# The HBM layout of a gate matrix G: by block of 32 tokens, expert row and expert against by expert row, expert and token

## The reference, cut to what matters

```python
va, ia = lax.top_k(sa, 16);  vb, ib = lax.top_k(sb, 16)       # 8 heads, product keys
top_s, pos = lax.top_k(va[..., :, None] + vb[..., None, :], 16)   # flattened over the pairs
experts = ia * 128 + ib                                        # the 8 * 16 = 128 picks of a token
gates = softmax(top_s)
act = gelu(einsum('tkd,td->tk', expert_u[experts], x))
out = einsum('tk,tkd->td', gates * act, expert_v[experts])
```

## Time and profile before

| what | value |
|---|---|
| median of three runs | 4338.44 us |
| the profiled execution, its own time | 4348.75 us |
| its span in the profile | 4346.7 us |
| mean granted TensorE clock | 0.906 of full speed |
| PE (TensorE) busy | 3666.6 us, 84% |
| DVE (VectorE) busy | 2812.8 us, 65% |
| POOL (GpSimd) busy | 1565.9 us, 36% |
| ACT (ScalarE) busy | 909.8 us, 21% |
| DMA queue q0 (issued by GpSimd) | 184336 packets, 666.53 MB, 41.1% of 16 engines' span |
| DMA queue q1 (issued by SP) | 194306 packets, 374.83 MB, 24.1% |

### The profile page before, as it was taken

One profiled execution on the slowest core, in us unless ns is written; L12 is line 12 of the kernel. 1 busy time (PEld: TensorE's weight loads), 2 busy tenths in 40 slices (PEclk: granted clock), 3 DMA queues, 4 the chain that ended last, 5 costly groups with the idle time before them and its releaser, 6 DMA issues.

```text
span 4346.7 us, 40408 instructions
## 1 busy us (share of the span) xinstructions
PE 3666.6 (84%) x13372; PEld 2071.1 (48%) x13372; DVE 2812.8 (65%) x5406; ACT 909.8 (21%) x1917; POOL 1565.9 (36%) x1400
## 2 busy tenths in 40 slices
PE   8999968888556667888569889999899899889995
PEld 6444435555343357788534334444344444434442
DVE  1222234567231127878858888888889888887777
ACT  0111114566211102554520111111011110111110
POOL 0000000000224200000036566657666667666765
PEclk9999986998768878898689999999999999999998
DMA  7122112110424245665189899999999999999997
GB/s 273 64 81 76 59 54 101 49 45 27 107 80 116 78 162 186 237 228 214 83 315 337 313 392 376 378 346 366 387 392 373 371 384 372 359 375 392 389 388 282
DMA packets 378849, 1043.93 MB, mean 240 GB/s; under 512 B 32685, under 2 KB 116041, under 8 KB 374482
## 3 DMA queue, kind: packets, MB, share of 16 engines
q0 software_dynamic: 184336, 666.53, 41.1%
q1 hardware_dynamic: 194306, 374.83, 24.1%
HBM read 973.80 MB, written 67.14 MB: 239 GB/s over the span
## 4 chain that ended last, share of the span: by engine, by line
DVE 15%; DMA 13%; PE 12%; POOL 4%; DVEq 4%; issue 3%; ACT 0%; SPq 0%; ACTq 0%
DMA pick_v<-in_expert_v,ids 9%; DVE acc L2438 7%; PE psY L2321 7%; PE psH L2308 5%; DVE e_junk L2422 4%; DMA e_u<-in_expert_u 4%; DVEq L2433 3%; POOL pick_u L2248 2%; POOL pick_v L2256 2%; PE psU L2300 1%; DVE e_away L1735 1%; DVE e_found L1738 1%; DVE e_W L2387 0%; DVE Y L2395 0%; DVEq L1701 0%
## 5 line engine op out<-in xcount | busy, mean ns | idle before, releaser
L2308 PE MATMUL psH<-XT,e_uT 128*128 128x512 f32 x2048 | 968.7, 615 | 86.1 <-ACT e_uT L2345 86.0
L2321 PE MATMUL psY<-e_v,e_W 128*128 128x512 f32 x2048 | 889.0, 595 | 20.4 <-DVE e_W L2387 12.1
L2438 DVE SCALAR_TENSOR_TENSOR acc<-pick_v,pick_w,acc 128x1024 f32<-128x1024 f32 x571 | 733.5, 1285 | 244.7 <-DMA pick_v<-in_expert_v,ids 184.0
L2248 POOL DMA_INDIRECT pick_u<-in_expert_u,ids x576 | 718.0, 1246 | 389.1 <-DVE pick_dot L2422 244.6
L2256 POOL DMA_INDIRECT pick_v<-in_expert_v,ids x576 | 667.4, 1159 | 287.6 <-issue 159.9
L2422 DVE CUSTOM_DVE_ANT_0 e_junk<-pick_u,x_rows 128x1024 bf16<-128x1024 f32 x576 | 702.5, 1220 | 24.8 <-DMA pick_u<-in_expert_u,ids 12.6
L2321 PEld LDWEIGHTS psY<-e_v,e_W 128*128 128x128 f32 x2048 | 390.7, 191 | 516.1 <-issue 497.7
L2308 PEld LDWEIGHTS psH<-XT,e_uT 128*128 128x128 f32 x2048 | 381.7, 198 | 479.8 <-issue 375.7
L363 PE MATMUL ps_p<-w_in_sb,hT 128*128 128x512 f32 x1008 | 443.2, 597 | 0.0
L2345 ACT ACTIVATE e_uT<-psU 128x512 f32<-128x512 f32 x256 | 149.2, 594 | 736.4 <-PE psU L2300 653.6
L363 PEld LDWEIGHTS ps_p<-w_in_sb,hT 128*128 128x128 f32 x1008 | 189.8, 191 | 233.4 <-issue 233.3
(11 more groups left out here) (450 smaller groups left out, 4071.1 us busy)
## 6 DMA issues: line engine op xcount, KB each, us to landing
w_query_sb<-in_w_query SPq DMA_DIRECT2D x36, 2048.0 KB, 8.5
e_u<-in_expert_u SPq DMA_DIRECT2D x128, 512.0 KB
e_v<-in_expert_v SPq DMA_DIRECT2D x128, 512.0 KB
G_d<-G_stage SPq DMA_DIRECT2D x16, 2048.0 KB, 9.8
e_g<-G_d SPq DMA_DIRECT2D x32, 1024.0 KB
w_ada<-in_w_ada POOLq DMA_DIRECT2D x16, 1024.0 KB, 5.9
w_in_sb<-in_w_in SPq DMA_DIRECT2D x7, 2048.0 KB, 19.1
pick_u<-in_expert_u,ids POOLq DMA_INDIRECT x576
```

What stands on the lines that cost most here:

```text
L2248: pool.indirect_dma_start(gu[:, i % NGU, :], None, io["expert_u"][0], bass.IndirectOffsetOnAxis(ids[:, q % 2, j:j + 1], 0)).then_inc(pu_in ...
L2308: m = pe.matmul(psH[a % 2][:, :], uT[:, a % 2, j, :], XT[:, j, :], start=j == 0, stop=j == KD - 1)
L2321: m = pe.matmul(psY[i % NY][:, :], W[:, (b * NBK + t) % NW, k * P:(k + 1) * P], v[:, t, half_cols(half)], start=t == 0, stop=t == NBK - 1)
L2438: dve.scalar_tensor_tensor(out=sums_q, in0=gv[:, i % NGV, :], scalar=wgt[:, m % 2, o:o + 1], in1=sums_q, op0=ALU.mult, op1=ALU.add).then_i ...
```

## The change

The order of the dimensions of G in HBM changes, from (block of 32 tokens, b, a, token) to (b, a, block of 32 tokens, token). A store from `G_stage` now writes, for each b and a, one piece of 32 tokens, 128 bytes; a load reads, for each b, 4 rows a of 512 tokens, 8 KB in one piece. The SBUF tensor `e_g` takes the same order, with the same size, and the operands of `weigh` become plain rows of 512.

```diff
-        G_d = dram("G_d", (TD // HT, P, NK, HT))
+        G_d = dram("G_d", (P, NK, TD // HT, HT))
@@ routing, keep (SP)
-                sp.dma_start(G_d[q], gs[:, q % NS_, :, :]).then_inc(g_stored[q % NS_], 16)
+                sp.dma_start(G_d[:, :, q, :], gs[:, q % NS_, :, :]).then_inc(g_stored[q % NS_], 16)
@@ apply
-        g = sb("e_g", [P, 2, TD // HT, GA, HT])
+        g = sb("e_g", [P, 2, GA, TD])
@@ apply, SP
-                    sp.dma_start(g[:, i % 2, :, :, :], G_d[:, :, a:a + GA, :].rearrange("q b a t -> b q a t")).then_inc(g_in[i % 2], 16)
+                    sp.dma_start(g[:, i % 2, :, :], G_d[:, a:a + GA, :, :].rearrange("b a q t -> b a (q t)")).then_inc(g_in[i % 2], 16)
@@ apply, weigh (DVE)
-                w = W[:, a % NW, :].rearrange("p (q t) -> p q t", t=HT)
-                dve.tensor_tensor(w, w, g[:, a // GA % 2, :, a % GA, :], ALU.mult).then_inc(weighed, 1)
+                w = W[:, a % NW, :]
+                dve.tensor_tensor(w, w, g[:, a // GA % 2, a % GA, :], ALU.mult).then_inc(weighed, 1)
```

## The result

The changed kernel takes 4352.61 us (median of 6 runs, 4341.66 to 4358.43) where the kernel before takes 4340.62 us on the same chip (6 runs, the three shown ahead among them). The ratio is 1.003, with a 95% interval of 1.0017 to 1.0043: 12 us slower, between 7 and 19. Timed again on another chip in the last group of experiments it was 1.0027 (1.0015 to 1.0038). The forecast was no change, 4338 us.

A forecast was written before the change was run, and what follows sets the result against it. The DMA engines' time was taken to bound the expert stage, TensorE and VectorE a little starved. -31 + 15 + 6 + 10 - 1 = -1 us: 4347.8 profiled, 4338 us median; own range 4320 to 4356, whole range 4290 to 4405.

The forecast's parts named there:

- The line through the packets: DMA packet price from 512-byte and 16 KB packets: 0.0386 ns per byte plus 7.7 ns, so 12.7 ns for 128 bytes.
- the choice of 20 ns: Price taken for a 128-byte packet in the stores of G, midway between 12.7 and 27.5 ns: 20.5 us a store.
- The tail: End of routing: the last store of G, without cover, grows from 5.1 to 20.5 us: +15 us.
- The pairs: Routing: two stores of G issued together, twice, delay the query weights behind them on q1: +6 and +10 us.
- SP's issue: Routing: SP's time to issue a store may grow with 16384 packets, but what follows would queue anyway: nothing.
- The loads: Expert stage: 32 loads of G each take 0.96 us less of all engines, counted in full: -31 us.
- a block that does not get shorter: Expert stage: the prediction is wrong if a block of 8 expert rows still takes 127 us.
- start of the stage: Expert stage: the first load of G delays the second e_u by some 1 us less: -1 us.
- Nothing gained in the expert stage: Rival: VectorE and its gathers set the expert stage's pace, the loads' saving is lost in slack: +31, 4369 us; chance 0.10.
- Cheap small packets: Rival: 128-byte packets cost what the line says, 13 us a store, only the tail left: -24, 4314 us; chance 0.29.
- The late e_u was the pace: Rival: each expert block's sums begin 6 us or more earlier, -96 instead of -31: 4272 us; chance 0.07.
- The case of a 128-byte write that costs as much as one of 512 bytes: Rival: stores become the bound of routing, 28 us a store or more: +38, 4376 us, up to 4478; chance 0.27.

The follow-up runs named there:

- e13: The changed kernel with all 16 stores of G issued by ScalarE instead of SP: 0.9998 of the kernel before, 4335.5 us.
- e2: The kernel before with only the loads of G changed, to runs of 8 KB (stores still 16 KB): 0.9978 of the kernel before, 4322.7 us.
- e15: The kernel of e2, unaltered, timed again in the last group: 0.9967 of the kernel before.
- e5: The kernel before with VectorE's scaled sum of each pick cut to 512 of 1024 columns, loads of G in 512 bytes: 0.9864, 4201.76 us.
- e6: The halved VectorE sum of e5 with loads of G in runs of 8 KB: 0.9802 of the kernel before, 4177.53 us.
- e8: The kernel before without the picks' gelu on ScalarE and its wait, loads of G in runs of 8 KB: 1.0014 of the kernel before.
- e9: G laid out by pairs of rows a, stores in runs of 256 bytes, loads of 8 KB: 0.9986 of the kernel before, 4252.04 us.
- e10: Stores of G in runs of 64 bytes, loads in runs of 512 bytes: 1.0272 of the kernel before, 4372.94 us.

## Why the prediction was right or wrong

The forecast was no change; the kernel got 12 us slower, which is inside the range given, 4290 to 4405, and near the upper end of the forecast's own. "Slower" had been given 0.42, more than the other two. By its steps:

- **The line through the packets** was nearly right, the choice of 20 ns was not. Runs of 64, 128, 256 and 512 bytes went at 87, 145, 218 and 290 GB/s: 11.8, 14.1, 18.8 and 28.2 ns for each packet and engine, a straight line of 9.4 ns and 0.0366 ns a byte, that ends at 609 ns for 16 KB (measured 0.64 us). The prediction's line from the earlier trace rows gave 12.7 ns for 128 bytes. I moved off it to 20 because of the earlier trace rows as an upper bound and of the earlier trace rows, a load in tiny runs that shares its start with others. That row was no evidence, and its sum was wrong too: 38 ns counts all the time of the 16 engines, and with their share of 0.77 it would have been 24.
- **The tail** was forecast at +15 and is +10.6 us. 14.5 us a store instead of 5.1 give 9.4 of them.
- **The pairs** were forecast at +6 and +10 and cost about 4 and 10, but that is in part luck: at 14.5 us a store the sum of that step gives nothing for the first and little for the second. What it left out is SP's issue, put at nothing since what follows would queue in any case. SP stands in the issue until the store ahead has nearly drained, so the query weights are asked for later, too (by 2 and 7 us). The two errors work against each other, and routing came to +23 where +31 had been summed. The trace shows the weights late behind the stores, and e13 shows that the cost goes when the stores leave SP; it does not separate the place on the queue from the time in the issue. The stores of the last step were taken to come every 27 us; they come 21 to 30 us apart, which 14.5 us a store still clears.
- **The loads** are the step that failed, and that made the forecast wrong in sign: with 10 us for them the sum would have been some 20 us slower. -31 us had been counted in full on the path "as the stage runs at the engines' limit". The price of the packets was about right: q1's share of the stage's 2100 us fell from 22.5% to 20.7%, 38 us of all engines, and a load of G is through in 4 us instead of 21 (medians, from its first packet to its last). But a share of 0.99 did not mean that the engines' time alone was the limit. 8 us came out in the change and 10 to 12.5 us with the loads alone (e2, e15), and these are 12 us of the first block, in which one late e_u was the pace. The fifteen blocks, which should have given nearly all of the 31, gave nothing: a block takes 130.1 us in the mean before and 130.3 after. The prediction had named a block that does not get shorter as a sign of being wrong. With VectorE's sums halved the blocks give 12 us (e5, e6), so VectorE's list is in the way; the term "start of the stage", put at -1, was where the gain lay. The prediction's reading of the earlier trace rows, that the time of a late e_u would only be passed on to VectorE, was right for the blocks, as the waits of e2 and e8 show, though not for the first one; it should have been applied to the engines' time as well as to TensorE's.
- **The rivals.** "Nothing gained in the expert stage", at 0.10, was the nearest to the expert stage and gave 4369 us, too high by the cheaper packets of routing and by the first block. "Cheap small packets", at 0.29, was nearly right on the packet (13 us a store) and wrong on the rest. "The late e_u was the pace", at 0.07, holds for the first block alone. The case of a 128-byte write that costs as much as one of 512 bytes did not come. The Trainium skill ("DMA: Bandwidth & Descriptors", Specifications) says that below 512 bytes the engine reads, modifies and writes. The traces disagree as far as time goes: the four sizes lie on one line with 16 KB, and no extra appears below 512 bytes. That such runs don't reach line rate is so, with 145 GB/s for 128 bytes; but 512 bytes, at 290, don't either, where stores of 16 KB go at some 410 (2 MB in 5.1 us). The fixed part per packet and the price per byte are enough for all five sizes. The Trainium skill's section "Why small descriptors are slow (HBM only)", on the same page, names a fixed overhead for each packet. Runs e9 and e10 agree that there is one, 9.4 ns on this line.

What stays open: why leaving out the picks' gelu costs 6 to 7 us, and how the fifteen blocks are paced. Relieving VectorE shortens them by 45 us and taking away the loads of G by 26, so neither VectorE's list nor the engines' time is the pace alone; TensorE is busy for 92% of the stage too, and no run relieved it. The profiles show many small waits of VectorE for gathers, none of which stands for it alone.

## What to carry to other kernels

When several engines of a stage are busy to 85% or 90% and the DMA share is near 1, the saving on one of them is worth what is left after the next one; take work away from the suspected pace setter and see whether the saving appears. Then cut the stage at the same instruction in both profiles and see where the saving lies: a total of 8 us, read as a little from each of sixteen blocks, was 12 us from the first. Price a transfer by its number of packets as well as its bytes, with a line through two sizes seen in the trace, and look at what stands behind it on the same queue and behind its issue in the program. A layout need not choose between writer and reader: in groups of 4 rows both runs are long (512 bytes and 8 KB), and it beat both kernels, 0.9984, 0.9979 and, with the stores on a queue of their own, 0.9978 of the kernel before.

## What the runs showed of the hardware that was not expected

An issue of a DMA by SP, mostly 0.3 to 0.7 us, took 14.4 us right behind a store of 16384 packets, and 24 us behind one of 32768. The same holds whatever is issued: the second store of a pair took 15 to 17 us itself (28 to 34 with 32768 packets), while a store with nothing close ahead took 0.5 to 1.2. The loads of 512 bytes do it on a small scale: the second e_u of the expert stage, issued behind the first load of G, took 7.58 us before and 0.7 with G in pieces of 8 KB (e13). ScalarE's issue of the stores took 0.5 to 0.6 us in thirteen of sixteen cases and 2.4 to 4.0 in three; its stores are at least 21 us apart. Routing with stores of 16 KB takes 646.2 to 646.5 us in seven profiles on several chips (the eighth, without the loads of G, has 643.2), while the phases ahead of it differ by 18 us between the two profiles laid side by side at the start, and by 75 us between groups (`r_gain` issued at 1457 us where the kernel before takes 4260 us, and at 1535 where it takes 4335): the difference between chips lies there, and only ratios within a group can be used.
